# Rotary part of the stream scores in mixer B as one product of 96 stacked rows

## The chip, the cores and the metric

One core of one Trainium2 chip. The metric is the device time of one execution in microseconds; the kernel before takes 1887.1 us (median of 3 runs, 1885.34 to 1888.52).

## The reference

Two layers of a streaming encoder run for a prompt of 512 tokens and for 8 running streams of 16 new tokens each, with shared weights. Each layer projects its input, runs two attention mixers, gates and adds them, and ends in a convolutional feed-forward part. The change touches one term of mixer B, for the streams alone: latent attention whose scores are the sum of a latent part and a rotary part.

```python
def _latent_attend(q_lat, q_rope, ckv, krope, mask):
    s = (jnp.einsum('bqhr,bkr->bhqk', q_lat, ckv) + jnp.einsum('bqhe,bke->bhqk', q_rope, krope)).astype(f32) * MLA_SCALE
    ...
    p = jax.nn.softmax(s, axis=-1).astype(ckv.dtype)
    return jnp.einsum('bhqk,bkr->bqhr', p, ckv)
```

For a stream the keys are 512 cached positions and the 16 new ones, `q_rope` and `krope` have 32 features, and 8 heads times 16 tokens give 128 queries.

## The kernel before

Everything is held with features on partitions: 512 prompt tokens and 8 x 16 stream tokens are 640 columns, taken in two halves of 320. Large matrix products are made in fp32r, TensorE's one-pass format, from parts: an operand is split into an upper part (a ScalarE copy to fp32r) and a lower part (the difference, on GpSimd for weights and on VectorE for activations), and three products upper x upper, lower x upper, upper x lower are added (`dense`, `gate_half`). The small products of attention are made in fp32, which TensorE runs as two instructions each.

The attention stage of a layer is a fixed list of 40 units, `UNITS`: 8 of mixer A for the prompt (`Ap`), 8 of mixer A for the streams (`As`, units 8 to 15), then eight times two prompt units of mixer B (`Bp`) and one stream unit of mixer B (`Bs`). So the `Bs` units are 18, 21, 24, 27, 30, 33, 36 and 39 (`BS_UNIT`); `AS_LAST` is 15. Each engine has its own loop over steps u, written out by hand:

- TensorE, step u: `scores(u + 2)`, `turn(u)` (transposes of the probabilities), the gate products that stand behind u (`gate_half`, 48 products of 320 columns for a gate; steps with u % 4 == 3 have none), `values(u - 1)`.
- VectorE, step u: `peaks(u + 2)` (row maxima), `turned_half(u)` (copies half of the transposes), `normalise(u + 1)`, `take_out(u - 1)`.
- ScalarE, step u: `turned_half(u)`, `exps(u + 2)`, `take_gate` and a copy of weights (`high`) for the gates behind u, now and then `ya_high`.
- The sync engine's queue: loads of cache rows (`load_cache(r)`), gate results out, weights in, in the order in which the quarters of the gates come. `load_cache(r)` waits for the scores of the stream before, since the key tile has one buffer.

A semaphore counts each hand-over: `scores_done`, `peak_ready`, `exp_ready`, `probs_ready`, `turned`, `out_done`. An engine that waits holds up all that stands behind in its loop.

In `scores`, kind `Bs` (L1848 to L1851): two fp32 products with `q_lat` (old keys 512 columns, new keys 16), and two fp32 products over 32 rows with the rotated queries, which lie in partitions 32 to 63 of tile `packed`: old keys from `krc_t`, 512 columns (L1850), and new ones.

```python
MM(old, q_lat[:, i, :], ckvc_t[:], start=True, stop=False)
MM(new, q_lat[:, i, :], ckv_t[:, s0:s0 + TDEC], start=True, stop=False)
MM(old, rot, krc_t[ROPE:2 * ROPE, :], start=False, stop=True)
ins = MM(new, rot, kr_r[:, s0:s0 + TDEC], start=False, stop=True)
```

Of the kernel before, what the change touches and what calls it, by code (L numbers as in the profile page):

```python
# [26 lines left out]
F32 = mybir.dt.float32  # L27
F32R = mybir.dt.float32r
ALU = mybir.AluOpType
ACT = mybir.ActivationFunctionType  # L30
AX = mybir.AxisListType.X

P = 128
DEPTH, D, SEQ, NREQ, TDEC, PAST, CHUNK, WINDOW = 2, 1024, 512, 8, 16, 512, 64, 128
TS = NREQ * TDEC
T = SEQ + TS
# [4 lines left out]
QL, KVL, ROPE, NOPE, VD = 384, 128, 32, 64, 64  # L41
# [102 lines left out]
NU = len(UNITS)  # L144
NAP = sum(x[0] == "Ap" for x in UNITS)
BS_UNIT = [u for u, x in enumerate(UNITS) if x[0] == "Bs"]
B_FIRST = min(u for u, x in enumerate(UNITS) if x[0][0] == "B")
AS_LAST = max(u for u, x in enumerate(UNITS) if x[0] == "As")
# [26 lines left out]
def build(nc, inp, out):  # L175
    ctx = ExitStack()
    with ctx:
# [31 lines left out]
        def place(name, at, shape, dt=F32):  # L209
            size = int(np.prod(shape[1:]))  # L210
            used[0] = max(used[0], at + size)
            with ExitStack() as s:
                if at:
                    s.enter_context(nc.sbuf_tensor("below_" + name, [P, at], F32))
                return s.enter_context(nc.sbuf_tensor(name, shape, dt))
# [7 lines left out]
        o = 8 * T  # L223
# [14 lines left out]
        vc = place("vc", o + NREQ * WINDOW, [P, NREQ, P])  # L238
        cq_lo = place("cq_lo", o, [P, KQ, T], F32R)
        ckvc_t = place("ckvc_t", o, [P, PAST])  # L240
        krc_t = place("krc_t", o + PAST, [P, PAST])
        ckvc = place("ckvc", o + 2 * PAST, [P, 2, PAST])
        o += 2 * NREQ * P
        k_t = place("k_t", o, [P, T])
        o += T
        v_tok = place("v_tok", o, [P, NB, P])
        ukc = place("ukc", o, [P, 4, KVL])
# [2 lines left out]
        packed = place("packed", o, [P, NREQ * P])  # L250
# [4 lines left out]
        ckv_t = place("ckv_t", o, [P, T])  # L255
        o += T
        kr_r = place("kr_r", o, [P, T])[ROPE:2 * ROPE, :]
        o += T
        bias_p = place("bias_p", o, [P, HEADS, WB])
        tab_sb = place("tab_sb", o, [HEADS, REL])  # L260
# [57 lines left out]
        def sem(name):  # L318
            return ctx.enter_context(nc.semaphore(name))
# [15 lines left out]
        sq_ready, rms_std, cq_scaled, cq_hi_ready, cq_lo_ready = (  # L335
            sem("sq_ready"), sem("rms_std"), sem("cq_scaled"), sem("cq_hi_ready"), sem("cq_lo_ready"))
        ckv_ready, kr_ready = sem("ckv_ready"), sem("kr_ready")
        rotating, qr_ready, exp_table = sem("rotating"), sem("qr_ready"), sem("exp_table")
        bs_loaded = sem("bs_loaded")
        mask_made, rows_loaded = sem("mask_made"), sem("rows_loaded")  # L340
# [34 lines left out]
        KF = KD - 2  # L375
        N_PAR = 12
        N_ROWS = 3


        gate_dram = nc.dram_tensor("gate_logits", (2 * KD, P, T), F32).ap()  # L380
# [59 lines left out]
        def row(t, j):  # L440

            if isinstance(j, int):
                return t[:, j, :]
            return t[:, bass.ds(j, 1), :].rearrange("p a n -> p (a n)")
# [10 lines left out]
        def _(sp):  # L455
# [23 lines left out]
            for layer in range(DEPTH):  # L479
# [149 lines left out]
                def load_cache(r):  # L629
                    sp.wait_ge(scores_done, layer * NU + (AS_LAST if r == 0 else BS_UNIT[r - 1]) + 1)  # L630
                    settle(sp)
                    if r >= 1:
                        sp.wait_ge(out_done, layer * NU + (AS_LAST if r == 1 else BS_UNIT[r - 2]) + 1)
                        settle(sp)
                    row = lambda name: inp[name][bass.ds(layer * NREQ + r, 1)].rearrange("a p n -> p (a n)")
                    sp.dma_start(ckvc[:, r % 2, :], row("ckvc")).then_inc(bs_loaded, 16)
                    sp.dma_start(ckvc_t[:], row("ckvc_t")).then_inc(bs_loaded, 16)
                    sp.dma_start(krc_t[ROPE:2 * ROPE, :], row("krc_t")).then_inc(bs_loaded, 16)


                for c in range(4 * NG):
# [119 lines left out]
        def _(act):  # L761
            A = act.activation
# [30 lines left out]
            for layer in range(DEPTH):  # L793
# [96 lines left out]
                def take_gate(g):  # L890

                    m = g // 2
                    if m >= 1:
                        act.wait_ge(gate_stored[g % 2], layer * (8 * NG) + 16 * m)
                    act.wait_ge(gate_done, layer * NG + g + 1)
                    A(logits[:, g % 2, :], ps[:, 7, 0:HT], ACT.Identity,  # L896
                      bias=vec[:, V_BG + m % 2 * KD + m // 2:V_BG + m % 2 * KD + m // 2 + 1]).then_inc(gate_taken, 1)
                    if g % 2 == 1:
                        high(S_GATE + 2 + m // 2, halves_=(m % 2,))

                def ya_high(k):
                    act.wait_ge(out_taken, layer * NU + AS_LAST + 1)
                    A(ya_hi[:, k, :], y_a[:, k, :], ACT.Copy).then_inc(ya_hi_ready, 1)

                take_gate(0)
                act.wait_ge(exp_table, layer + 1)
                exps(0)
# [2 lines left out]
                for u in range(NU):  # L910
                    turned_half(u)
                    if u + 2 < NU:
                        exps(u + 2)
                    for g in gate_behind(u):
                        take_gate(g)
                    if u in YA_HIGH:
                        ya_high(YA_HIGH.index(u))


                ya_high(3)  # L920
# [174 lines left out]
        def _(dve):  # L1095
# [41 lines left out]
            for layer in range(DEPTH):  # L1137
# [191 lines left out]
                for u in range(NU):  # L1329
                    if u + 2 < NU:  # L1330
                        peaks(u + 2)
                    if u >= NAP:
                        turned_half(u)
                    if u + 1 < NU:
                        normalise(u + 1)


                    if u == 1:
                        dve.wait_ge(rotated_stored, (layer + 1) * 64)
                        dve.wait_ge(kv_stored, (layer + 1) * 32)  # L1340
                    if u >= 1:
                        take_out(u - 1)
                    if u - 1 in YA_HIGH:
                        ya_low(YA_HIGH.index(u - 1))
# [255 lines left out]
                for k in range(2):  # L1600
                    n = before_norm(J_DN2, k)
                    r = res_of[1][:, k, :]
# [22 lines left out]
        def _(pe):  # L1625
# [7 lines left out]
            for layer in range(DEPTH):  # L1633
# [175 lines left out]
                def scores(u):  # L1809
                    kind, i, g = UNITS[u]  # L1810
                    b = u % 2
                    bank = 2 * b
                    if u >= 2:
                        pe.wait_ge(exp_ready, layer * NU + u - 1)
                    if u == B_FIRST:
                        pe.wait_ge(kr_ready, layer + 1)
                        pe.wait_ge(rows_loaded, layer * (16 * N_ROWS) + 16 * N_ROWS)
                        pe.wait_ge(rotated_loaded, (layer + 1) * 64)
                    if kind == "Ap":
                        n = P if i == 0 else WB  # L1820
                        k0 = (i + 1) * P - n
                        for t in range(2):
                            for gg in range(GROUPS):
                                gp = slice(gg * HD, (gg + 1) * HD)
                                ins = MM(ps[:, bank + gg, t * WB:t * WB + n], q_a[gp, 2 * g + t, i * P:(i + 1) * P],
                                         k_t[gp, k0:k0 + n], start=True, stop=True)
                    elif kind == "As":
                        if i == 0:
                            pe.wait_ge(par_loaded, layer * (16 * N_PAR) + 16 * N_PAR)
                        settle(pe)  # L1830
                        s0 = SEQ + i * TDEC
                        for gg in range(GROUPS):
                            gp = slice(gg * HD, (gg + 1) * HD)
                            lhs = q_a[gp, i // 2, SEQ + (i % 2) * GH * TDEC:SEQ + (i % 2 + 1) * GH * TDEC]
                            MM(ps[gp, bank, 0:WINDOW], lhs, kc_t[gp, i, :], start=True, stop=True)
                            ins = MM(ps[gp, bank, WINDOW:SKEYS], lhs, k_t[gp, s0:s0 + TDEC], start=True, stop=True)
                    elif kind == "Bp":
                        n = (i + 1) * P
                        for k in range(2):
                            h = 2 * g + k  # L1840
                            ins = MM(ps[:, bank + k, 0:n], qb[0:KB, h, i * P:(i + 1) * P], kb[0:KB, h, 0:n],
                                     start=True, stop=True)
                    else:
                        s0 = SEQ + i * TDEC
                        pe.wait_ge(bs_loaded, layer * (48 * NREQ) + 48 * (i + 1))
                        old, new = ps[:, bank, 0:PAST], ps[:, bank + 1, 0:TDEC]
                        rot = q_rs[:, i, :, :].rearrange("p h n -> p (h n)")
                        MM(old, q_lat[:, i, :], ckvc_t[:], start=True, stop=False)  # L1848
                        MM(new, q_lat[:, i, :], ckv_t[:, s0:s0 + TDEC], start=True, stop=False)
                        MM(old, rot, krc_t[ROPE:2 * ROPE, :], start=False, stop=True)  # L1850
                        ins = MM(new, rot, kr_r[:, s0:s0 + TDEC], start=False, stop=True)  # L1851
                    ins.then_inc(scores_done, 1)

# [356 lines left out]
```

## Time and profile before

| | us |
|---|---|
| median of 3 runs | 1887.1 |
| the profiled execution | 1887.02 |
| its span | 1885.2 |
| TensorE busy | 1843.2 |
| VectorE busy | 1010.5 |
| ScalarE busy | 655.1 |
| GpSimd busy | 540.6 |

The profile is of one execution. Its busy times overlap: an engine that is busy for a small share can still be the one that others wait for at one place. The products of TensorE are pipelined, so one lasts longer in the table than the distance to the next; what a product costs is the distance from its start to the next start. The granted clock of TensorE is 0.994 of full in the mean. The two layers run the same program; the second layer's attention stage stands 928.2 us behind the first one's.

### The profile page before, as it was taken

The numbers are of one execution on the slowest core, as the hardware profiler recorded it, in microseconds if no ns is written. First come the engines' busy times: TensorE is split into PE (matmuls) and PEld (weight loads), VectorE is DVE, ScalarE is ACT, GpSimd is POOL, SyncE is SP. The second block draws the span as 40 slices with busy tenths as digits, with TensorE's granted clock in tenths as the row PEclk, the third lists the DMA queues.
The fourth block names the chain that finished last, engine by engine and source line by source line (L and its number), as shares of the span: only waits on it lengthen the run. The fifth ranks groups of instructions, "written<-read, shape, count | busy, mean of one in ns | idle before, by whom it ended". The sixth has DMA issues, their size and how long they took to land. (4 is left out here: it accounts for less than half of the span.)

```text
span 1885.2 us, 31852 instructions
## 1 busy us (share of the span) xinstructions
PE 1843.2 (98%) x12458; PEld 1752.6 (93%) x12458; DVE 1010.5 (54%) x1597; ACT 655.1 (35%) x1381; POOL 540.6 (29%) x244
## 2 busy tenths in 40 slices
PE   8999999999999999999999999999999999999996
PEld 8987887999999999999999888889999999999995
DVE  3576544359754333444776765444696443244447
ACT  4245443333433212332322644333334331133323
POOL 2331211134143244333422322112323333443331
PEclk9999999999999999999999999999999999999998
DMA  7262322321121122211242623214211211222121
GB/s 227 100 163 70 127 84 89 125 107 68 68 90 61 67 73 90 89 50 56 89 137 71 157 76 121 92 64 145 102 68 68 89 56 67 82 85 89 42 75 57
DMA packets 67003, 171.20 MB, mean 91 GB/s; under 512 B 16376, under 2 KB 33456, under 8 KB 59056
## 3 DMA queue, kind: packets, MB, share of 16 engines
q1 hardware_dynamic: 66896, 169.72, 27.4%
q8 instruction: 74, 1.21, 0.3%
q14 instruction: 33, 0.27, 0.1%
HBM read 152.47 MB, written 19.61 MB: 91 GB/s over the span
## 5 line engine op out<-in xcount | busy, mean ns | idle before, releaser
L719 POOL TENSOR_TENSOR w_lo<-w_raw,w_hi 128x1024 fp32r<-128x1024 f32 (+2 forms) x230 | 530.3, 2314 | 1270.6 <-ACT w_hi L806 1251.4
L806 ACT ACTIVATE w_hi<-w_raw 128x1024 fp32r<-128x1024 f32 (+2 forms) x228 | 218.3, 975 | 438.1 <-PE ps L1668 431.8
L1668 PE MATMUL ps<-x_hi,w_hi 128*128 128x320 f32 x1408 | 321.6, 309 | 0.0
L1668 PE MATMUL ps<-x_hi,w_lo 128*128 128x320 f32 x1408 | 320.7, 309 | 0.0
L1668 PE MATMUL ps<-x_lo,w_hi 128*128 128x320 f32 x1408 | 320.7, 309 | 0.0
L1668 PEld LDWEIGHTS ps<-x_hi,w_hi 128*128 128x128 f32 x1408 | 235.4, 188 | 0.3
L1668 PEld LDWEIGHTS ps<-x_lo,w_hi 128*128 128x128 f32 x1408 | 235.5, 188 | 0.0
L1668 PEld LDWEIGHTS ps<-x_hi,w_lo 128*128 128x128 f32 x1408 | 235.3, 188 | 0.0
L1568 DVE TENSOR_SCALAR f_conv<-f_ext,vec 128x656 f32<-128x656 f32 x44 | 63.9, 1452 | 202.9 <-ACT tail L1036 200.5
L1935 PE MATMUL ps<-x_hi,w_hi 128*128 128x320 f32 x512 | 163.6, 319 | 1.5 <-ACT logits L896 1.5
L1935 PE MATMUL ps<-x_hi,w_lo 128*128 128x320 f32 x512 | 158.3, 309 | 0.0
L1935 PE MATMUL ps<-x_lo,w_hi 128*128 128x320 f32 x512 | 158.1, 309 | 0.0
L1668 PE MATMUL ps<-hf_hi,w_hi 128*128 128x320 f32 x624 | 143.0, 310 | 0.0
L1668 PE MATMUL ps<-hf_lo,w_hi 128*128 128x320 f32 x624 | 142.3, 309 | 0.0
L1668 PE MATMUL ps<-hf_hi,w_lo 128*128 128x320 f32 x624 | 142.3, 309 | 0.0
L1583 DVE TENSOR_TENSOR hf_lo<-f_h,hf_hi 128x640 f32 x44 | 83.9, 1906 | 46.8 <-ACT hf_hi L1044 46.8
L1668 PEld LDWEIGHTS ps<-hf_hi,w_hi 128*128 128x128 f32 x624 | 104.7, 188 | 0.3
L1668 PEld LDWEIGHTS ps<-hf_hi,w_lo 128*128 128x128 f32 x624 | 104.7, 188 | 0.0
L1668 PEld LDWEIGHTS ps<-hf_lo,w_hi 128*128 128x128 f32 x624 | 104.6, 188 | 0.0
L1935 PEld LDWEIGHTS ps<-x_hi,w_hi 128*128 128x128 f32 x512 | 96.3, 188 | 3.1 <-ACT logits L896 2.4
L1935 PEld LDWEIGHTS ps<-x_lo,w_hi 128*128 128x128 f32 x512 | 96.4, 188 | 0.0
L1935 PEld LDWEIGHTS ps<-x_hi,w_lo 128*128 128x128 f32 x512 | 96.1, 188 | 0.0
(298 smaller groups left out, 3191.2 us busy)
## 6 DMA issues: line engine op xcount, KB each, us to landing
w_raw<-in_slabs SPq DMA_DIRECT2D x84, 1024.0 KB, 4.9
w_raw<-in_slabs SPq DMA_DIRECT2D x20, 768.0 KB, 4.0
gate_logits<-logits SPq DMA_DIRECT2D x64, 160.0 KB, 1.9
gates<-gate_logits SPq DMA_DIRECT2D x16, 640.0 KB, 6.4
w_raw<-in_slabs SPq DMA_DIRECT2D x16, 640.0 KB, 3.8
ckvc<-in_ckvc SPq DMA_DIRECT2D x16, 256.0 KB, 2.7
ckvc_t<-in_ckvc_t SPq DMA_DIRECT2D x16, 256.0 KB, 3.0
w_raw<-in_slabs SPq DMA_DIRECT2D x6, 512.0 KB, 5.9
```

Of the source, the lines that this page charges most:

```text
L719: pool.tensor_tensor(to, w_raw[:, s % 2, c], hi.bitcast(F32), ALU.subtract).then_inc(wlo_ready, 1)
L806: A(w_hi[:, s % 2, c], w_raw[:, s % 2, c], ACT.Copy).then_inc(whi_ready, 1)
L1568: link(TSC(f_conv[:, 0:NC_], f_ext[:, 2:EXT], w(2), vec[:, bass.ds(V_CB + j, 1)], ALU.mult, ALU.add))
L1583: TT(row(hf_lo, jj), f_h[:], row(hf_hi, jj).bitcast(F32), ALU.subtract).then_inc(fh_lo_ready, 1)
L1668: ins = MM(out_[:, a, :], w, x[:, t, a * HT:(a + 1) * HT], start=t == 0 and w is wh and x is hi, stop=t == tiles - 1 and w is wl)
L1935: ins = MM(ps[:, 7, 0:HT], w, x[:, t, a * HT:(a + 1) * HT], start=t == 0 and w is wh and x is x_hi, stop=t == KD - 1 and w is wl)
```

## The change

The rotary product with the old keys (L1850) is made in fp32r from parts, and the three products of parts are stacked into one: queries in partitions 0 to 31 upper, 32 to 63 lower, 64 to 95 upper; keys upper, upper, lower. One product over 96 rows adds all three.

- Tile `q_stack` (all streams, 1024 columns) is made once per layer: three ScalarE copies of 32x1024 (`q_stack_highs`, in ScalarE's step 14, unit 18 minus 4) and a subtraction on VectorE (step 15).
- The keys of stream r are loaded three times (partitions 0 to 31 and 32 to 63 of `krc_raw`, and `krc_copy` in partitions 64 to 95): two more DMAs per stream. ScalarE copies 64x512 in place and 32x512 (`krc_highs`, at the end of step "unit minus 4"); VectorE subtracts 32x512 in step "unit minus 3", behind `normalise`.
- TensorE waits for `krc_ready` before the scores of a stream, and for `q_stack_ready` before those of stream 0.

```diff
--- before.py
+++ after.py
@@ -238,10 +238,14 @@
         vc = place("vc", o + NREQ * WINDOW, [P, NREQ, P])
         cq_lo = place("cq_lo", o, [P, KQ, T], F32R)
         ckvc_t = place("ckvc_t", o, [P, PAST])
-        krc_t = place("krc_t", o + PAST, [P, PAST])
+
+
+        krc_raw = place("krc_raw", o + PAST, [P, PAST])
+        krc = place("krc", o + PAST, [P, PAST], F32R)
         ckvc = place("ckvc", o + 2 * PAST, [P, 2, PAST])
         o += 2 * NREQ * P
         k_t = place("k_t", o, [P, T])
+        q_stack = place("q_stack", o, [P, NREQ * P], F32R)
         o += T
         v_tok = place("v_tok", o, [P, NB, P])
         ukc = place("ukc", o, [P, 4, KVL])
@@ -255,6 +259,7 @@
         ckv_t = place("ckv_t", o, [P, T])
         o += T
         kr_r = place("kr_r", o, [P, T])[ROPE:2 * ROPE, :]
+        krc_copy = place("krc_copy", o, [P, T])[2 * ROPE:3 * ROPE, 0:PAST]
         o += T
         bias_p = place("bias_p", o, [P, HEADS, WB])
         tab_sb = place("tab_sb", o, [HEADS, REL])
@@ -335,6 +340,8 @@
         sq_ready, rms_std, cq_scaled, cq_hi_ready, cq_lo_ready = (
             sem("sq_ready"), sem("rms_std"), sem("cq_scaled"), sem("cq_hi_ready"), sem("cq_lo_ready"))
         ckv_ready, kr_ready = sem("ckv_ready"), sem("kr_ready")
+        krc_high, krc_ready, q_stack_high, q_stack_ready = (
+            sem("krc_high"), sem("krc_ready"), sem("q_stack_high"), sem("q_stack_ready"))
         rotating, qr_ready, exp_table = sem("rotating"), sem("qr_ready"), sem("exp_table")
         bs_loaded = sem("bs_loaded")
         mask_made, rows_loaded = sem("mask_made"), sem("rows_loaded")
@@ -375,6 +382,7 @@
         KF = KD - 2
         N_PAR = 12
         N_ROWS = 3
+        N_CACHE = 80
 
 
         gate_dram = nc.dram_tensor("gate_logits", (2 * KD, P, T), F32).ap()
@@ -635,7 +643,8 @@
                     row = lambda name: inp[name][bass.ds(layer * NREQ + r, 1)].rearrange("a p n -> p (a n)")
                     sp.dma_start(ckvc[:, r % 2, :], row("ckvc")).then_inc(bs_loaded, 16)
                     sp.dma_start(ckvc_t[:], row("ckvc_t")).then_inc(bs_loaded, 16)
-                    sp.dma_start(krc_t[ROPE:2 * ROPE, :], row("krc_t")).then_inc(bs_loaded, 16)
+                    for to in (krc_raw[0:ROPE, :], krc_raw[ROPE:2 * ROPE, :], krc_copy):
+                        sp.dma_start(to, row("krc_t")).then_inc(bs_loaded, 16)
 
 
                 for c in range(4 * NG):
@@ -902,6 +911,20 @@
                     act.wait_ge(out_taken, layer * NU + AS_LAST + 1)
                     A(ya_hi[:, k, :], y_a[:, k, :], ACT.Copy).then_inc(ya_hi_ready, 1)
 
+                def q_stack_highs():
+
+                    act.wait_ge(rotated_loaded, (layer + 1) * 64)
+                    act.wait_ge(scores_done, layer * NU + AS_LAST + 1)
+                    rot = packed[ROPE:2 * ROPE, :]
+                    A(q_stack[0:ROPE, :], rot, ACT.Copy)
+                    A(q_stack[2 * ROPE:3 * ROPE, :], rot, ACT.Copy)
+                    A(q_stack[ROPE:2 * ROPE, :], rot, ACT.Copy).then_inc(q_stack_high, 1)
+
+                def krc_highs(r):
+                    act.wait_ge(bs_loaded, layer * (N_CACHE * NREQ) + N_CACHE * (r + 1))
+                    A(krc[0:2 * ROPE, :], krc_raw[0:2 * ROPE, :], ACT.Copy)
+                    A(krc[2 * ROPE:3 * ROPE, :], krc_copy, ACT.Copy).then_inc(krc_high, 1)
+
                 take_gate(0)
                 act.wait_ge(exp_table, layer + 1)
                 exps(0)
@@ -915,6 +938,10 @@
                         take_gate(g)
                     if u in YA_HIGH:
                         ya_high(YA_HIGH.index(u))
+                    if u + 4 in BS_UNIT:
+                        if u + 4 == BS_UNIT[0]:
+                            q_stack_highs()
+                        krc_highs(BS_UNIT.index(u + 4))
 
 
                 ya_high(3)
@@ -1333,6 +1360,15 @@
                         turned_half(u)
                     if u + 1 < NU:
                         normalise(u + 1)
+                    if u + 3 in BS_UNIT:
+                        if u + 3 == BS_UNIT[0]:
+                            dve.wait_ge(q_stack_high, layer + 1)
+                            part = q_stack[ROPE:2 * ROPE, :]
+                            TT(part, packed[ROPE:2 * ROPE, :], part.bitcast(F32), ALU.subtract).then_inc(q_stack_ready, 1)
+                        r = BS_UNIT.index(u + 3)
+                        dve.wait_ge(krc_high, layer * NREQ + r + 1)
+                        part = krc[2 * ROPE:3 * ROPE, :]
+                        TT(part, krc_copy, part.bitcast(F32), ALU.subtract).then_inc(krc_ready, 1)
 
 
                     if u == 1:
@@ -1842,12 +1878,16 @@
                                      start=True, stop=True)
                     else:
                         s0 = SEQ + i * TDEC
-                        pe.wait_ge(bs_loaded, layer * (48 * NREQ) + 48 * (i + 1))
+                        pe.wait_ge(bs_loaded, layer * (N_CACHE * NREQ) + N_CACHE * (i + 1))
+                        pe.wait_ge(krc_ready, layer * NREQ + i + 1)
+                        if i == 0:
+                            pe.wait_ge(q_stack_ready, layer + 1)
                         old, new = ps[:, bank, 0:PAST], ps[:, bank + 1, 0:TDEC]
                         rot = q_rs[:, i, :, :].rearrange("p h n -> p (h n)")
                         MM(old, q_lat[:, i, :], ckvc_t[:], start=True, stop=False)
                         MM(new, q_lat[:, i, :], ckv_t[:, s0:s0 + TDEC], start=True, stop=False)
-                        MM(old, rot, krc_t[ROPE:2 * ROPE, :], start=False, stop=True)
+
+                        MM(old, q_stack[0:3 * ROPE, i * P:(i + 1) * P], krc[0:3 * ROPE, :], start=False, stop=True)
                         ins = MM(new, rot, kr_r[:, s0:s0 + TDEC], start=False, stop=True)
                     ins.then_inc(scores_done, 1)
```

ScalarE, steps 14 and 15 of a layer, from the copy of gate weights on (`w_hi`); `probs_t` are copied transposes, `probs,st_sum` exponentials. Before:

```order
L806 ACTIVATE w_hi<-w_raw 128x1024
L888 ACTIVATE probs_t<-ps 128x128
L874 ACTIVATE probs,st_sum<-ps,st_nm 128x128 x2
L888 ACTIVATE probs_t<-ps 128x128
L878 ACTIVATE probs,st_sum<-ps,st_nm 128x528
```

With the change:

```order
L815 ACTIVATE w_hi<-w_raw 128x1024
L919 ACTIVATE q_stack<-packed 32x1024
L920 ACTIVATE q_stack<-packed 32x1024
L921 ACTIVATE q_stack<-packed 32x1024
L925 ACTIVATE krc<-krc_raw 64x512
L926 ACTIVATE krc<-krc_copy 32x512
L897 ACTIVATE probs_t<-ps 128x128
L883 ACTIVATE probs,st_sum<-ps,st_nm 128x128 x2
L897 ACTIVATE probs_t<-ps 128x128
L887 ACTIVATE probs,st_sum<-ps,st_nm 128x528
```

Five copies now stand between the weight copy and the transposes of unit 15, and the exponentials of unit 17 behind them.

VectorE, step 15, from the row maxima of unit 17 (`st_mx`) over normalising unit 16 (`probs`) to the maxima of unit 18. Before:

```order
L1277 TENSOR_REDUCE st_mx<-ps 128x2
L1281 TENSOR_SCALAR st_nm<-st_mx 128x2
L1301 COPY probs_t<-ps 16x128
L1290 RECIPROCAL st_ri<-st_sum 128x2
L1294 TENSOR_SCALAR probs<-probs,st_ri 128x128 x2
L1312 COPY y_a<-ps 64x4x16
L1318 COPY y_a<-ps 64x4x16
L1280 TENSOR_REDUCE st_mx<-ps 128x1
```

With the change:

```order
L1304 TENSOR_REDUCE st_mx<-ps 128x2
L1308 TENSOR_SCALAR st_nm<-st_mx 128x2
L1328 COPY probs_t<-ps 16x128
L1317 RECIPROCAL st_ri<-st_sum 128x2
L1321 TENSOR_SCALAR probs<-probs,st_ri 128x128 x2
L1367 TENSOR_TENSOR q_stack<-packed,q_stack 32x1024
L1371 TENSOR_TENSOR krc<-krc_copy,krc 32x512
L1339 COPY y_a<-ps 64x4x16
L1345 COPY y_a<-ps 64x4x16
L1307 TENSOR_REDUCE st_mx<-ps 128x1
```

The two subtractions stand behind the normalising of unit 16 and ahead of `take_out(14)`; at the other streams only the one of `krc` comes.

TensorE, the last instructions of step 21 and the scores of a stream in step 22, with the change:

```order
L1952 MATMUL ps<-probs_t,v_b 64x128 x6
L1887 MATMUL ps<-ckvc_t,q_lat 128x512
L1888 MATMUL ps<-ckv_t,q_lat 128x16
L1890 MATMUL ps<-krc,q_stack 128x512
L1891 MATMUL ps<-kr_r,packed 128x16
L1909 MATMUL ps<-ident,probs 128x128 x8
```

The third product was `ps<-krc_t,packed`, at the same place.

## Rows read from the trace of the kernel before

**Rows 1.** The page, busy time of each engine over the span
```profile
PE 1843.2 (98%) x12458; PEld 1752.6 (93%) x12458; DVE 1010.5 (54%) x1597; ACT 655.1 (35%) x1381; POOL 540.6 (29%) x244
```

**Rows 2.** Timeline of TensorE: start, us, engine, line, operation, tiles, shape, count [idle before]
```profile
205.12 1.12 PE L1848 MATMUL ps<-ckvc_t,q_lat 128*128 128x512 f32 x2
...
206.30 1.12 PE L1850 MATMUL ps<-krc_t,packed 32*128 32x512 f32 x2
207.26 0.28 PE L1851 MATMUL ps<-kr_r,packed 32*128 32x16 f32 x2
207.88 0.44 PE L1869 MATMUL ps<-ident,probs 128*128 128x128 f32 x2 [0.34 <-DVE probs L1294]
208.08 0.39 PE L1935 MATMUL ps<-x_hi,w_hi 128*128 128x320 f32 x1
208.31 0.31 PE L1935 MATMUL ps<-x_lo,w_hi 128*128 128x320 f32 x1
208.45 0.31 PE L1935 MATMUL ps<-x_hi,w_lo 128*128 128x320 f32 x1
```

**Rows 3.** Groups by line and shape, VectorE and ScalarE: busy us, mean ns
```profile
L1120 DVE TENSOR_TENSOR third_z<-w_raw,third_z 128x512 fp32r<-128x512 f32 x4 | 2.6, 685 | 0.0
...
L1120 DVE TENSOR_TENSOR w_lo<-w_raw,w_hi 128x1024 fp32r<-128x1024 f32 x4 | 4.9, 1224 | 1.4 <-ACT w_hi L773 1.4
...
L1160 DVE TENSOR_TENSOR kr_t<-ps,sin_k 32x640 f32<-32x640 f32 x2 | 1.6, 816 | 0.1
...
L842 ACT ACTIVATE kb<-ps 64x512 f32<-64x512 f32 x8 | 4.7, 592 | 30.5 <-PE ps L1774 30.5
```

**Rows 4.** Timeline of ScalarE before stream 0
```profile
203.56 1.05 ACT L806 ACTIVATE w_hi<-w_raw 128x1024 fp32r<-128x1024 f32 x1
204.57 0.28 ACT L888 ACTIVATE probs_t<-ps 128x128 f32<-128x128 f32 x1
```

**Rows 5.** The instructions of tile krc_t: its DMA (ns to issue, first and last start), landing
```profile
L638 SPq DMA_DIRECT2D krc_t<-in_krc_t x16: 416/429/644, 198.7 to 1246.5; - x16
...
DMA to landing us min/median/max: 2.8/2.9/6.3
```

**Rows 6.** Timeline of VectorE before stream 0
```profile
204.81 2.24 DVE L1281 TENSOR_SCALAR st_nm<-st_mx 128x2 f32<-128x2 f32 x1
...
207.75 0.21 DVE L1312 COPY y_a<-ps 64x64 f32<-64x64 f32 x1
```

**Rows 7.** Timeline of TensorE at stream 4
```profile
269.73 1.13 PE L1848 MATMUL ps<-ckvc_t,q_lat 128*128 128x512 f32 x2
```

**Rows 8.** Timeline of VectorE before stream 4
```profile
270.41 0.75 DVE L1294 TENSOR_SCALAR probs<-probs,st_ri 128x384 f32<-128x384 f32 x2
271.07 0.28 DVE L1318 COPY y_b<-ps 128x128 f32<-128x128 f32 x1
```

**Rows 9.** Timeline of TensorE at streams 1 and 2
```profile
222.24 1.13 PE L1848 MATMUL ps<-ckvc_t,q_lat 128*128 128x512 f32 x2
...
236.94 1.12 PE L1848 MATMUL ps<-ckvc_t,q_lat 128*128 128x512 f32 x2
```

**Rows 10.** Timeline of VectorE before streams 1 and 2
```profile
219.08 2.11 DVE L1294 TENSOR_SCALAR probs<-probs,st_ri 128x128 f32<-128x128 f32 x2
...
235.78 0.62 DVE L1294 TENSOR_SCALAR probs<-probs,st_ri 128x256 f32<-128x256 f32 x2
```

**Rows 11.** Stretches: us, busy time of the five engines, granted clock, DMA share, GB/s
```profile
140.00:170.00 30.00, 28.64 (x219) 23.57 (x219) 21.56 (x58) 18.26 (x57) 5.25 (x3) 1.00 0.17 58
...
350.00:355.00 5.00, 2.49 (x11) 2.43 (x10) 3.72 (x5) 4.12 (x6) 0.00 (x0) 0.72 0.85 331
```

**Rows 12.** Timeline of TensorE: the longest waits of the attention stage
```profile
149.65 1.09 PE L1869 MATMUL ps<-ident,probs 128*128 128x128 f32 x8 [1.36 <-DVE probs L1294]
...
352.60 0.87 PE L1668 MATMUL ps<-yb_hi,w_hi 128*128 128x320 f32 x2 [2.51 <-DVE yb_lo L1353]
...
355.82 0.46 PE L1668 MATMUL ps<-yb_hi,w_hi 128*128 128x320 f32 x2
```

## The prediction

> **What bounds the kernel now.** I read the page's busy times first: TensorE is busy for 98% of the span, so time is saved by taking work from TensorE, and lost wherever it must wait longer [rows 1]. The change acts only in the attention stage (about 127 to 345 us in the first layer, and the same 928.2 us later in the second), so next I went through that stage's timeline engine by engine. TensorE runs there a hand-written order: in step u it does the scores of unit u+2, the transposes of unit u, mostly one gate of 48 products as filler, and the values of unit u-1. One step in four (u = 3, 7, 11, ...) has no gate. The stream-score units, named stream 0 to 7 here, are units 18, 21, ..., 39; their scores stand in step "unit minus 2". Little waiting is left: at stream 0 the transposes wait 0.34 us, in rows 2.
>
> **What the change takes off TensorE.** The old product of 32 rows and 512 columns starts at 206.30 and the next one at 207.26: 0.96 us in two instructions [rows 2]. It becomes one fp32r product. No fp32r product of 512 columns stands in the trace. The 320-column ones start 0.14 to 0.15 us apart, that is 0.133 us of columns at 2.4 GHz and 0.014 us besides; the first one behind fp32 work takes 0.23, so 0.08 us more for the switch [rows 2]. I take 0.213 + 0.014 + 0.08 = 0.31 us. Bounds: 0.23 (no switch cost) and 0.96 (no gain at all). So a product saves 0.65 us, and 16 of them 10.4 us; with the lower bound 11.7. That it now has 96 rows in place of 32 I cost at nothing: the fp32 product of 128 rows, from 205.12, has the same spacing as the one of 32.
>
> The Trainium skill (TensorE: Matmul & The Clock Gate, section "Back-to-back issue gap") gives 131 ns as the sustained spacing of 512-column products, against the spacing of rows 2, which is longer for only 320 columns; by the page the sum would come out some 2.9 us lower (16 x 0.18), and I go by the rows.
>
> **What it adds on ScalarE, VectorE and the queue.** Per layer, once: three ScalarE copies of 32x1024 and one VectorE subtraction of 32x1024. Per stream: two ScalarE copies (64x512, 32x512), one VectorE subtraction of 32x512, and two more DMAs. Cost goes by columns, not by partitions: a VectorE operation of 32x640 takes 816 ns, between 685 for 128x512 and 1224 for 128x1024 [rows 3]. So the subtractions cost 1.22 and 0.685 us. ScalarE needs 1.01 us from one 1024-column copy to the next instruction [rows 4], and about 0.55 for 512 columns (592 ns busy, rows 3, the tail of which the next one overlaps). The queue issues two DMAs more per stream at 0.43 to 0.64 us each: 1.1 us. What counts is not this work but where it stands: TensorE may start a stream's scores only when VectorE has made the low parts, and VectorE makes them one step earlier, behind normalising unit "minus 2" of that stream.
>
> **Stream 0 (step 16).** ScalarE is through with the weight copy at 204.57 [rows 4]. Now three copies come (to 207.6) and the two key copies (to 208.7). The keys have landed by then: issued at 198.7, at most 6.3 to land, 1.1 for the added issues, makes 206.1 [rows 5]. VectorE is through with normalising unit 16 at 207.75, late because the operation from 204.81 took 2.24 us [rows 6]; then 1.22 + 0.685 bring it to 209.65. Both inputs of that chain come in step 15, which has no gate, so TensorE has nothing to fill with: today it starts these scores at 205.12 [rows 2]. It will wait **4.5 us**. The scores last 2.42 us now (205.12 to 207.54) and then 2.42 - 0.65 = 1.77 us, to 211.45; the transposes that start at 207.88 today start 3.55 us later. Queued behind the waiting instruction is all of TensorE's work, so this goes to the end of the kernel. ScalarE's step 15, its copy of transposes and exponentials of unit 17, moves by 4 us too, but is wanted only in steps 16 and 17, behind the wait.
>
> **Stream 4 (step 28).** Step 27 again has no gate. TensorE starts the scores at 269.73 today [rows 7]; VectorE normalises unit 28 from 270.41 to 271.07 [rows 8] and only then does the new subtraction, to 271.75. TensorE waits **2.0 us**, and after the shorter product is 1.37 us later than today.
>
> **The other six.** A gate stands in the step before, and covers the subtraction. The tightest are stream 1, where VectorE is through at 219.08 + 2.11 + 0.685 = 221.9 and TensorE comes at 222.24, and stream 2, where 235.78 + 0.62 + 0.685 = 237.1 stands against 236.94, a wait of 0.15 us [rows 9, 10]. If that cover shrank by 0.5 us, two streams per layer would wait. The remaining four have a margin of over 1 us. Their gain is six times 0.65 = 3.9 us per layer. The 1.1 us of queue time delays weight loads that are issued some 10 us before their use: nothing.
>
> **The clock.** At the end of the attention stage TensorE waits 2.51 us, and the granted clock falls to its low level, 1.2 GHz: 0.72 mean in 350 to 355 us [rows 11, 12]. From 352.60 to 355.82 six pairs of products run that take 6 x 0.293 = 1.76 us at the full clock: 1.46 us lost [rows 12]. A wait of 1.36 us, before 149.65, left the clock full in its stretch (1.00) [rows 11, 12]. The new wait at stream 0 is 4.5 us, longer than the one that sent the clock down, so I add 1.5 us per layer; bounds 0 and 3. The 2.0 us at stream 4 lies between the two, nearer to 2.51 but amid fp32 products; I take no fall there. The Trainium skill (same page, section "HAM oscillation") warns of just this, gaps that put the next burst on the low clock; the trace agrees, at the 2.51 us above.
>
> **Sum.** Per layer: stream 0 +3.55, its clock +1.5, stream 4 +1.37, stream 2 +0.15, six gains -3.9: +2.67 us. Two layers: +5.3. The profiled execution took 1887.0 (span 1885.2 and 1.8 around it), the median of the runs is 1887.1, so both give **1892.3 us**.
>
> **Rivals.**
> A. *The clock stays full through the 4.5 us.* For it: the fall seen came behind 16 small products, not behind gates, and one place per layer is little evidence. Against: it came in both layers, after barely more than half the idle time. Then 1887.0 + 2.3 = 1889.3, not slower beyond what can be told: this is the one on the other side. It decides from the point at which a wait of 4.5 us no longer lowers the grant.
> B. *It falls at stream 4 too.* The wait of 2.0 us is 0.5 short of one that did it. Another 1.5 us per layer: 1895.3.
> C. *The stacking is hidden and only the shorter product shows.* It would need VectorE and ScalarE to handle 32 partitions faster than 128, or low parts made earlier than I read. 1887.0 - 10.4 = 1876.6. The 816 ns of the 32-partition row speaks against it, as does the order, which puts the subtraction behind the normalising.
> D. *The product is not shorter* (a 96-row fp32r product behind fp32 ones costs as before, so the change doesn't do what it says). Then 5.3 + 10.4: 1902.7. Each gate begins with such a switch and costs 0.08 us, which speaks against it.
>
> **How the numbers follow.** A measurement of this kernel tells about 0.2% (3.8 us) from no change: slower is over 1890.9, faster under 1883.3. Forecast 0.50, A 0.22, B 0.18, C 0.05, D 0.02, other mishaps 0.03. The forecast's own spread is about 2 us (0.5 us on each of two stalls, 0.05 on each product, 1 on the clock, all twice), so a fifth of it falls under 1890.9. Faster: C, 0.05. Same: A nearly whole and 0.1 of the forecast, 0.31. Slower: the rest, 0.64. The range takes in A and B with a margin of 1.5 to 2 us, 1887.3 to 1897.0, and leaves out C, D and the mishaps' ends. 1892.3 is the likeliest case.
>
> **What would show it.** In the profile after: the fp32r product with 96 rows, 16 of them, next start about 0.31 us later; a TensorE wait of some 4.5 us before the scores of stream 0 and some 2.0 before stream 4, in each layer, both put down to VectorE's subtraction; none over 0.5 at the other streams; a stretch of granted clock near 0.5 behind stream 0's wait. The forecast is wrong if VectorE's subtraction of 32x1024 takes well under 1.2 us, if the wait at stream 0 is under 3 us, if the clock stays full, or if streams 1 and 2 wait too.

## The result and the profile after

| | before | with the change |
|---|---|---|
| median, us | 1887.81 (4 runs) | 1902.46 (4 runs) |
| ratio, with 95% interval | 1 | 1.008 (1.0066 to 1.0094) |
| span of the profiled execution, us | 1885.2 | 1900.1 |
| its mean granted clock | 0.994 | 0.987 |

The changed kernel is 14.7 us slower, against 5.3 forecast and a range that ended at 1897.0. The direction was right, the size was not. TensorE's busy time is as before [rows 1], although the new products save some of it:

```profile
PE 1843.4 (97%) x12442; PEld 1754.9 (92%) x12442; DVE 1021.8 (54%) x1615; ACT 679.7 (36%) x1419; POOL 540.5 (28%) x244
```

Of what it waited for, three lines of the list of waits (us in total, times, longest):

```profile
PE ps L1887 <- DVE krc L1371: 14.7, 6, 4.9
PE ps L1909 <- DVE probs L1321: 6.6, 8, 1.4
PE ps L1704 <- DVE yb_lo L1389: 5.0, 2, 2.5
```

The first line is new: 14.7 us in six waits, three in each layer. They are 4.90 us at stream 0, 2.22 at stream 4, 0.23 at stream 2. Stream 0 on TensorE's timeline (to be read beside rows 2):

```profile
209.93 2.04 PE L1887 MATMUL ps<-ckvc_t,q_lat 128*128 128x512 f32 x2 [4.90 <-DVE krc L1371]
...
212.05 0.77 PE L1890 MATMUL ps<-krc,q_stack 96*128 96x512 f32 x1
...
214.04 0.47 PE L1975 MATMUL ps<-x_lo,w_hi 128*128 128x320 f32 x1
214.31 0.47 PE L1975 MATMUL ps<-x_hi,w_lo 128*128 128x320 f32 x1
```

After the wait everything runs at the low clock: the pair of fp32 products from 209.93 takes 1.83 us to the next start where it took 0.96, and gate products are 0.27 us apart, not 0.147. ScalarE and VectorE before it (rows 4 and 6 before):

```profile
204.47 1.06 ACT L919 ACTIVATE q_stack<-packed 32x1024 fp32r<-32x1024 f32 x1
...
207.69 0.63 ACT L925 ACTIVATE krc<-krc_raw 64x512 fp32r<-64x512 f32 x1
208.33 0.62 ACT L926 ACTIVATE krc<-krc_copy 32x512 fp32r<-32x512 f32 x1
```

```profile
207.70 1.22 DVE L1367 TENSOR_TENSOR q_stack<-packed,q_stack 32x1024 fp32r<-32x1024 f32 x1
208.99 0.68 DVE L1371 TENSOR_TENSOR krc<-krc_copy,krc 32x512 fp32r<-32x512 f32 x1
```

ScalarE's two key copies end at 208.95, VectorE's subtraction begins at 208.99 and ends at 209.67, and TensorE starts at 209.93. The chain is the one that was forecast, to 0.1 us in each link but two: ScalarE's key copies take 0.63 and 0.62 us, not 0.55, and are through only just in time for VectorE's second subtraction; and 0.25 us pass from the end of that to TensorE's start. At stream 1 the clock is full again:

```profile
229.48 1.13 PE L1887 MATMUL ps<-ckvc_t,q_lat 128*128 128x512 f32 x2
...
230.59 0.47 PE L1890 MATMUL ps<-krc,q_stack 96*128 96x512 f32 x1
230.99 0.39 PE L1891 MATMUL ps<-kr_r,packed 32*128 32x16 f32 x2
231.31 0.44 PE L1909 MATMUL ps<-ident,probs 128*128 128x128 f32 x2
```

The new product costs 0.40 us to the next start (230.59 to 230.99), the one of before 0.96. The whole of a stream's scores takes 1.83 us (229.48 to 231.31) against 2.36 before (from 222.24, rows 9, to the next transposes at 224.60): 0.53 us less. The start of those transposes, before:

```profile
224.60 0.44 PE L1869 MATMUL ps<-ident,probs 128*128 128x128 f32 x2
```

The granted clock in the stretches around the two long waits is the column behind the busy times (us, busy time of PE, PEld, DVE, ACT, POOL, clock, DMA share, GB/s):

```profile
205.00:210.00 5.00, 0.10 (x2) 0.10 (x1) 4.81 (x9) 4.89 (x10) 1.86 (x1) 0.71 0.06 23
210.00:215.00 5.00, 5.00 (x14) 3.49 (x15) 1.69 (x7) 1.04 (x4) 0.00 (x0) 0.50 0.01 3
215.00:220.00 5.00, 5.00 (x28) 4.76 (x27) 0.33 (x3) 0.64 (x3) 0.00 (x0) 0.76 0.00 0
...
275.00:280.00 5.00, 2.78 (x16) 1.56 (x14) 2.90 (x8) 1.83 (x5) 0.00 (x0) 0.88 0.00 0
280.00:285.00 5.00, 5.00 (x21) 4.96 (x22) 2.24 (x6) 1.17 (x3) 0.00 (x0) 0.50 0.00 0
285.00:290.00 5.00, 5.00 (x29) 4.18 (x29) 0.29 (x1) 1.47 (x2) 1.16 (x1) 0.94 0.06 4
```

TensorE is busy for all of 210 to 220 us and of 280 to 290, and yet the clock is at its low level (0.50, that is 1.2 GHz) for about 10.2 us from 207 us on, and for about 6.8 us from 279 us on. (A mean of 0.71 over 5 us is 2.9 us at the low level, and so on.) The first stretch begins inside the wait, so 7.4 us of it (209.93 to about 217.3) are TensorE's working time; the second begins when TensorE is at work again, and all of it is.

One thing went the other way. At the end of the attention stage the clock fell before, and in this execution it does not. Before, and with the change:

```profile
345.00:360.00 15.00, 12.49 (x83) 11.96 (x84) 7.22 (x10) 8.21 (x12) 0.00 (x0) 0.89 0.56 203
```

```profile
355.00:370.00 15.00, 12.49 (x95) 12.09 (x94) 8.25 (x11) 9.36 (x13) 0.61 (x1) 1.00 0.65 227
```

How much later each stream's scores begin with the change than before, in the first layer (us; starts read from TensorE's timeline; all of them include that this execution was 0.17 us ahead when the stage reached stream 0):

| stream | 0 | 1 | 2 | 3 | 4 | 5 | 6 | 7 |
|---|---|---|---|---|---|---|---|---|
| later by | 4.81 | 7.24 | 7.01 | 6.43 | 8.19 | 10.70 | 10.15 | 9.61 |

From stream 0 to stream 1, 2.43 us are lost though nothing waits: 0.53 gained by the product, and the 0.34 us for which the transposes waited before is swallowed by the new wait, so 2.43 + 0.53 + 0.34 = 3.3 us are lost to the low clock. From 4 to 5 it is 2.51, so 3.0. Where neither a wait nor the clock disturbs, each stream gives back 0.53 to 0.58. With the last stream's gain (0.53) and the vanished fall at the stage's end (1.46, rows 12) the layer's loss is 4.98 + 2.43 - 0.23 - 0.58 + 1.76 + 2.51 - 0.55 - 0.54 - 0.53 - 1.46 = 7.8 us. Stream 0 of the second layer begins 12.86 us later than before; less its own 4.98 that leaves 7.9, where the first layer's 7.8 less the 0.17 make 7.6: the sum holds to 0.3 us. The second layer's shifts give 7.4 in the same way, and with the 0.17 us taken off the two layers make 15.0 of the spans' 14.9 us.

### The profile page after: what moved, and what is told of

The parts are those of the page before. It is cut to its first block and busy times, and to the rows that moved or that the text cites. A ratio compares the mean times of both kernels' runs of the same rounds, so it can differ in the third digit from the quotient of the medians.

```text
span 1900.1 us, 31912 instructions
## 1 busy us (share of the span) xinstructions
PE 1843.4 (97%) x12442; PEld 1754.9 (92%) x12442; DVE 1021.8 (54%) x1615; ACT 679.7 (36%) x1419; POOL 540.5 (28%) x244
```

## The experiments

Theory W: the loss is TensorE's waits for the low parts at streams 0 and 4 and the low clock behind each. Theory L: it is the added load, the copies, subtractions and DMAs, or the fp32r product itself. The first four runs move work or change the product's kind.

**e1: all the work of the change, earlier at streams 0 and 4.**

The main lines of the edit, shortened; `EARLY` is `(0, 4)`:

```diff
 # sync engine: cache of stream 0 ahead of a weight load
+                    if c + 1 == quarter_at_scores(AS_LAST):
+                        load_cache(0)
...
 # ScalarE, in step u
+                    if u + 4 == BS_UNIT[0]:
+                        krc_highs(0)
                     for g in gate_behind(u):
                         take_gate(g)
...
-                        if u + 4 == BS_UNIT[0]:
-                            q_stack_highs()
+                    if u + 5 == BS_UNIT[0]:
+                        q_stack_highs()
+                    if u + 4 in BS_UNIT[1:]:
                         krc_highs(BS_UNIT.index(u + 4))
...
 # VectorE, in step u, behind normalise(u + 1)
+                    if u + 4 == BS_UNIT[0] and 0 in EARLY:
+                        q_stack_low()
...
 # VectorE, behind take_out(u - 1)
+                    if u + 4 in BS_UNIT and BS_UNIT.index(u + 4) in EARLY:
+                        krc_low(BS_UNIT.index(u + 4))
```

> All the work of the change is kept, only its place differs. Stream 0: the cache load is issued ahead of a weight load, ScalarE copies q_stack one step earlier and the keys before it takes the gate, VectorE subtracts q_stack and keys in step 14. Stream 4: VectorE subtracts the keys at the end of step 26. Theory W (the loss is TensorE's waits of 4.9 and 2.2 us per layer at streams 0 and 4 and the low clock that follows each, some 3.1 us each): both waits under 0.3 us, clock full through the stage except at its end, where the fall of the kernel before returns, 16 products at 0.55 us less: 1887.8 - 8.5 = about 1879 to 1881 us. Theory L (the loss is the added load itself: copies, subtractions, DMAs, or the 96-row fp32r product pulls the clock down wherever it stands): the low-clock stretches stay in number, and the time falls by the waits alone, 14 us at most from 1902.5, so 1888 us or more.

Measured: 1881.19 us, ratio to before 0.9975 (0.9965 to 0.9984). So the same work, placed otherwise, is 21 us faster than the change, and faster than before. Theory L, which set 1888 as the least, falls. Of the 8.5 us that were forecast as gain 2.8 are missing (beside these runs the kernel before took 1886.87). The profile shows where, first in the first layer's waits, on VectorE and on GpSimd:

```profile
PE ps L1922 <- DVE probs L1326: 1.9, 2, 1.4
...
PE ps L1900 <- DVE krc L1364: 0.2, 1, 0.2
```

```profile
206.09 2.50 DVE L1326 TENSOR_SCALAR probs<-probs,st_ri 128x128 f32<-128x128 f32 x2
```

```profile
205.97 2.34 POOL L731 TENSOR_TENSOR w_lo<-w_raw,w_hi 128x1024 fp32r<-128x1024 f32 x1 [8.61 <-ACT w_hi L818]
```

Two instructions that take 0.48 us in the change take 2.50: they stand beside GpSimd's subtraction, which has moved onto them with ScalarE's later weight copy, and the transposes of unit 16 wait 1.37 us, in each layer, where they waited 0.34. In the first layer the clock stays full through this; in the second one it falls for some 3 us:

```profile
200.00:240.00 40.00, 38.39 (x248) 33.23 (x247) 24.36 (x63) 21.70 (x55) 7.15 (x3) 1.00 0.42 134
...
1136.00:1176.00 40.00, 39.22 (x250) 34.21 (x249) 20.76 (x56) 19.20 (x48) 7.16 (x3) 0.96 0.40 125
```

The Trainium skill (SBUF — State Buffer, section "Who interferes with whom") says that VectorE and GpSimd can lock each other out of a pair of ports they share, for a whole instruction; the trace agrees, with VectorE's pair of instructions ending at 208.59 us, behind GpSimd's at 208.31.

The parts add up to about what is missing: twice 1.03 us of added wait here, twice 0.23 at stream 2, and some 1.6 us of clock in the second layer, less 1.5 us because in that layer the clock does not fall at the end of the stage.

**e2 and e3: one place at a time.** e2 has e1's edits for stream 0 alone, e3 the one for stream 4 alone:

```diff
+EARLY = (0,)    # e2; e3: (4,), with the sync engine and ScalarE as in the change
...
+                    if u + 4 in BS_UNIT and BS_UNIT.index(u + 4) in EARLY:
+                        krc_low(BS_UNIT.index(u + 4))
```

> As e1 for stream 0, stream 4 as in the change. W: the wait before stream 0 and the 10.2 us stretch of low clock behind it go, the wait of 2.2 us and the 6.8 us stretch behind stream 4 stay; 1902.5 - 2 x (4.9 + 3.1) = 1886.5 us, up to 1889.5 if the fall at the end of the stage returns. L: low clock also at stream 0, 1892 us or more.

> As e1 for stream 4 only, stream 0 as in the change. W: wait and low clock stay at stream 0 and go at stream 4: 1902.5 - 2 x (2.2 + 3.2) = 1891.7 us, up to 1894.6 if the fall at the end of the stage returns. L: the time falls by 4.4 us at most, 1898 us or more.

Measured: e2 1889.98 us (1.0017, 1.0007 to 1.0026), e3 1893.86 us (1.0039, 1.0025 to 1.0053). Waits and two stretches, e2 and then e3:

```profile
PE ps L1900 <- DVE krc L1364: 4.7, 3, 2.2
```

```profile
200.00:240.00 40.00, 38.39 (x237) 33.33 (x235) 23.36 (x59) 21.26 (x54) 7.16 (x3) 0.96 0.39 127
265.00:300.00 35.00, 32.78 (x205) 26.65 (x204) 15.37 (x39) 14.73 (x35) 4.72 (x2) 0.95 0.25 79
```

```profile
PE ps L1896 <- DVE krc L1360: 10.3, 4, 4.9
```

```profile
200.00:240.00 40.00, 35.10 (x211) 30.36 (x210) 20.13 (x54) 19.38 (x46) 5.80 (x3) 0.91 0.46 144
265.00:300.00 35.00, 35.00 (x232) 28.66 (x231) 17.14 (x44) 17.72 (x39) 7.09 (x3) 1.00 0.30 96
```

Each place carries its own wait and its own low clock. Taking stream 0's away is worth 12.5 us, taking stream 4's away 8.6, together 21.1, and e1, which takes both, gains 21.3 on the change. e2 lies 0.5 us above its expectation's upper figure, e3 inside. What each gains beyond its waits, 12.5 - 9.8 = 2.7 and 8.6 - 4.4 = 4.2 us, is the clock. Taken off it are the waits of 1.38 us that e2 has as e1 has them, with a low clock of some 3 us behind the one in the first layer (0.96 above), and the fall at the stage's end, which is back in one layer of e2 and in both of e3.

**e4: the stacked product in fp32.**

```diff
-MM(old, q_stack[0:3 * ROPE, i * P:(i + 1) * P], krc[0:3 * ROPE, :], start=False, stop=True)
+MM(old, q_stack[0:3 * ROPE, i * P:(i + 1) * P].bitcast(F32), krc[0:3 * ROPE, :].bitcast(F32), start=False, stop=True)
```

> The change with all its copies, loads, subtractions and waits, but the product over the 96 stacked rows made in fp32 (two instructions) in place of fp32r. W: the waits stay 4.9 and 2.2 us; each of 16 products costs 0.53 to 0.55 us more, on the low clock more: 1902.5 + 9 = about 1911 to 1912 us. L (the fp32r product is what lowers the clock): the low stretches shrink, 1905 us or less.

Measured: 1914.25 us (1.0138, 1.0121 to 1.0155), 11.8 above the change and 2 above its expectation. Stream 1 at the full clock:

```profile
229.79 1.10 PE L1890 MATMUL ps<-krc,q_stack 96*128 96x512 f32 x2
230.82 0.39 PE L1891 MATMUL ps<-kr_r,packed 32*128 32x16 f32 x2
```

The product costs 1.03 us to the next start and in fp32r 0.40, so 0.63 x 16 = 10 us of it is the product. The four runs lie apart (1909.89 to 1918.18 us, mean clock 0.989 to 0.984, where the change has 0.987 and 0.988), so the other 2 us are within what the clock varies; they are not traced further. So the change does what it says: its product is short, and it is not what lowers the clock, which falls behind all four long waits with the fp32 product too.

**e6: the gate ahead of the scores in steps 16 and 28.** Nothing but TensorE's order changes; the late low parts stay late.

```diff
+                    if u + 2 in (BS_UNIT[0], BS_UNIT[4]):
+                        for g in gate_behind(u):
+                            gate_half(2 * g)
+                            gate_half(2 * g + 1)
                     if u + 2 < NU:
                         scores(u + 2)
                     turn(u)
+                    if u + 2 not in (BS_UNIT[0], BS_UNIT[4]):
                         for g in gate_behind(u):
```

> The change as it is on ScalarE, VectorE and the queue; TensorE alone does its gate ahead of the scores in steps 16 and 28. Theory W: the gate (3.6 us) covers the 2.2 us wait of stream 4 whole and leaves 1.3 us of the 4.9 at stream 0, without a long stretch of low clock: 1887 + 2 x 1.5 - 8.5 = about 1881 to 1884 us. Rival (the late low parts delay VectorE and ScalarE themselves, and the wait turns up at the next transposes): 1890 us or more.

Measured: 1881.83 us (0.9975, 0.9965 to 0.9985). In the first layer's stage TensorE now waits:

```profile
PE ps L1887 <- DVE krc L1371: 1.5, 2, 1.3
```

The 7.3 us have become 1.5, and the clock is 1.00 in both places in both layers; the first layer's:

```profile
200.00:240.00 40.00, 38.34 (x243) 32.59 (x242) 23.78 (x61) 22.63 (x54) 7.20 (x3) 1.00 0.47 149
265.00:300.00 35.00, 35.00 (x232) 28.58 (x232) 18.27 (x43) 15.83 (x36) 4.73 (x2) 1.00 0.28 93
```

Of the 20.6 us gained on the change 11.7 are the waits, and some 9 the clock, although the fall at the end of the stage is back in both layers.

**e7: e1 and the gate first in step 16.**

> e1 with one thing more: in step 16 TensorE does its gate ahead of the scores of stream 0 and the transposes of unit 16, so that the 1.37 us wait for VectorE's normalising (held up beside GpSimd) is covered too. Theory W: no wait over 0.3 us at streams 0 to 7, clock full in the stage up to its end; 16 products at 0.53 us less make 8.5, stream 2's wait costs 0.5 back: 1886.9 - 8 = about 1879 us. Rival theory L, weakened form (the added work costs some 2 us per layer wherever it stands): 1882 us or more, with no wait or low clock to show for it.

Measured: 1879.09 us (0.9956, 0.9943 to 0.997), the best of all: 8 us under before and 23 under the change. Waits in the first layer's stage, and two stretches:

```profile
PE ps L1922 <- DVE probs L1326: 0.6, 1, 0.6
...
PE ps L1900 <- DVE krc L1364: 0.2, 1, 0.2
```

```profile
200.00:240.00 40.00, 39.61 (x254) 34.09 (x253) 25.11 (x66) 22.41 (x56) 7.24 (x3) 1.00 0.42 134
265.00:300.00 35.00, 35.00 (x235) 28.24 (x234) 17.50 (x44) 17.08 (x39) 4.72 (x2) 1.00 0.28 91
```

No wait for the low parts is left but the 0.2 us at stream 2, and the clock is full. From stream 1 to stream 7 its lead over the kernel before grows from 0.08 to 2.96 us in the first layer and from 3.32 to 6.23 in the second, that is 0.48 us a stream (stream 2's wait included). 16 products at half a microsecond are 8 us, the gain of the medians (between the two profiled executions it is 7.1). Theory L's weakened form, 1882 or more, falls as well.

**e5 and r1 to r3: what the length of the low clock hangs on.** In e5 both waits are kept, but the gate comes right behind them and the fp32 scores after it.

```diff
+                    if u + 2 == BS_UNIT[0]:
+                        pe.wait_ge(krc_ready, layer * NREQ + 1)
+                        pe.wait_ge(q_stack_ready, layer + 1)
+                    if u + 2 == BS_UNIT[4]:
+                        pe.wait_ge(krc_ready, layer * NREQ + 5)
+                    if u + 2 in (BS_UNIT[0], BS_UNIT[4]):
+                        for g in gate_behind(u):
...
```

> Both waits are kept whole (TensorE waits for the low parts at the same points), but behind them comes the gate, fp32r products of 320 columns, before the fp32 scores and transposes. Theory F (fp32 products and transposes behind a wait do not bring the clock back, gate products do): the low stretch behind stream 0 shrinks from 10.2 to 3.4 to 6.8 us and the one behind stream 4 from 6.8 to 3.4 or none: 1902.5 - 2 x (1.7 to 4) = 1895 to 1899 us. Rival theory P (the length hangs on the wait and on when it falls, not on what follows): stretches as in the change, about 1902 us.

> The changed kernel unaltered, one more profiled execution, to see how far the stretches of low clock vary from execution to execution. Theory F (what follows the wait decides): 10.2 us behind stream 0 and 6.8 us behind stream 4 again. Theory P (it hangs on when the wait falls): other lengths, as e3 and e4 had 6.8 us and 6.8 to 13.7 us behind the same wait.

> As r1, a third profiled execution of the changed kernel: F the same lengths, P others.

> e5 once more (the waits kept, the gate right behind them). F: 3.4 to 6.8 us of low clock behind stream 0, at most 3.4 behind stream 4, under every layer's sum of the changed kernel. P: sums that overlap with those of the changed kernel.

Measured: e5 1897.46 us (1.0056, 1.004 to 1.0071), its repeat r3 1898.7 in one run; the changed kernel again 1903.42 (r1) and 1903.17 (r2). e5's waits and stretches, then r1's stretches:

```profile
PE ps L1975 <- DVE krc L1371: 13.6, 4, 4.7
```

```profile
200.00:240.00 40.00, 35.15 (x209) 30.72 (x208) 19.75 (x53) 19.19 (x46) 5.60 (x3) 0.91 0.46 144
265.00:300.00 35.00, 32.88 (x219) 27.00 (x218) 16.17 (x38) 16.46 (x36) 6.10 (x3) 1.00 0.30 96
```

```profile
200.00:240.00 40.00, 35.10 (x202) 30.46 (x201) 18.91 (x54) 19.09 (x47) 4.75 (x2) 0.87 0.45 142
265.00:300.00 35.00, 32.78 (x206) 27.87 (x204) 14.72 (x36) 15.09 (x34) 4.75 (x2) 0.95 0.27 91
```

The waits are 13.6 us in four places against 14.2 for the same four in the change, so of the 5 us gained over 4 are the clock's, although the fall at the stage's end is back in both layers. Behind stream 0 the changed kernel has 0.87 over 40 us in all three executions and both layers; e5 and r3 have 0.91 in all four. Behind stream 4 the change has 0.90, 0.95 and 0.95 in the first layer (0.91 in the second, over 40 us), e5 and r3 have 1.00, and in the second layer 0.96 and 1.00. Worked out from the streams' shifts as above, the clock costs 3.9 us behind stream 0 in the first layer of r1 and r2, where it was 3.3, and 1.5 behind stream 4, where it was 3.0. At stream 4, then, gate products right behind the wait went with a shorter low stretch than the same layer of the change has, or with none, in four layers of four. At stream 0 the order separates nothing: e3 has the wait and the order of the change there and 0.91 in both layers, as e5 has, and e4 has 0.91 in one layer and 0.83 in the other. In e5 and r3 stream 4 also comes earlier than in the change. So what follows the wait may be one cause and when the wait falls another; how they share the length was not settled.

## Why the prediction was wrong

Per layer, in us, forecast and measured (the first layer of the changed kernel):

| term | forecast | measured |
|---|---|---|
| wait at stream 0 | 4.5 | 4.9 |
| wait at stream 4 | 2.0 | 2.2 |
| wait at stream 2 | 0.15 | 0.23 |
| clock behind stream 0 | 1.5 | 3.3 |
| 0.34 us of waiting at stream 0, swallowed | -0.34 | -0.34 |
| clock behind stream 4 | 0 | 3.0 |
| eight shorter products | -5.2 | -4.3 |
| fall at the end of the stage | not considered | -1.5 |

**The step that failed** is "The clock". It took the price of a fall from the only one seen, 1.46 us, where fp32r products came right behind the wait, and carried it to a place where fp32 scores and transposes come first. There the clock stayed low for 10.2 us, 7.4 of them with TensorE at work, and cost 3.3 us; whether the fp32 work is the reason stays open. And it let the 2.0 us wait at stream 4 pass without a fall, where the runs show one in every execution of the changed kernel, in the profiled one for 3.0 us. Rival B had that fall, with 0.18, but at the same price, so its 1895.3 was too low as well. The two clock terms are short by 4.8 us per layer, 9.6 in all, where 9.4 were missing; the smaller errors (waits +0.7, product +0.9, the vanished fall -1.5 per layer) cancel, by luck: nothing ties them together.

**The waits** were right, in their places, their cause and nearly their size. The chain over ScalarE's copies, VectorE's normalising and its two subtractions was confirmed link by link, and by e1, e6 and e7, which take the waits away. What was missing is the time from the end of the subtraction to TensorE's start, about 0.25 us. Streams 1, 3, 5, 6 and 7 are covered, as forecast.

**The product** was taken at 0.31 us and costs 0.40, and its neighbours moved a little too; the saving is 0.53 per stream and not 0.65. The 131 ns of the Trainium skill (TensorE: Matmul & The Clock Gate, section "Back-to-back issue gap") would have been farther off than the 0.31. That its 96 rows cost nothing holds nearly: e4's fp32 product of 96 rows takes 1.03 us, that of 32 rows 0.96.

**The rivals.** A (clock stays full) did not come. C (the whole gain shows) did not come with this placement, but e7 is nearly that: 8 us under before. D (product not shorter) gives 1902.7, next to what was measured, and is wrong all the same: the time alone would have taken it for right; the 0.40 us and e4 show that it is not.

## What to carry to other kernels

Where TensorE is busy 98% of the time, a change that takes work from it but hangs it on a new chain of other engines is priced by where the chain ends, not by how much work it holds: the same copies and subtractions made this kernel 14.7 us slower or 8 us faster. Put filler work that needs nothing in front of the instruction that waits, above all in steps that have no other filler. And count a wait of over 2 us at more than its length, since the low clock behind it cost 1.5 to 3.9 us where it came, and it came behind every such wait that had fp32 scores behind it.

## What the runs showed of the hardware

- Around a wait of 4.9 us the granted clock was at its low level for 10.2 us, 7.4 of them behind the wait, with TensorE busy all through; behind the 2.2 us wait it fell about a microsecond after the work had begun again, for 6.8 us (in the first layer of r1 and r2 for about half of that, 0.95 over 35 us).
- A fall is no fixed property of a place: the wait of 2.5 us at the end of the stage let the clock fall in both layers before, in neither layer of the profiled execution of the change, and in one of two in r1 and r2. Of the four waits of 1.37 to 1.39 us at the same transposes in e1 and e2, two went without a fall; behind the other two, in the second layer of e1 and the first of e2, the clock was low for some 3 us.
- An fp32r product of 96 rows and 512 columns between fp32 ones costs 0.40 us to the next start, against 0.213 us of columns at 2.4 GHz.
- A ScalarE copy of 32x1024 takes 1.06 us and a VectorE subtraction of it 1.22, as for 128 partitions.
